# Two bank sets for the mLSTM numerators, output weights converted ahead of use, a three-stage input pipeline and later state products in a hybrid attention and mLSTM layer

## The reference

```python
h = rmsnorm(x, norm_g)
proj = h @ w_in                       # 2048 x 6672: aq ak av az | mq mk mv mo mz gates
# group A: 8 query heads on 2 key/value heads of 128, rmsnorm of q and k, axial rotary,
#          softmax(q k^T / sqrt(128)) v, times silu(az)
# group B: 4 mLSTM heads (q, k: 128, v: 256), chunks of 128 tokens, forward and backward;
#   num = (q k^T * w) v + si * (q C);  den = rowsum + si * (q n)
#   hd  = num / max(|den|, exp(-m));   C = sc * C + (we * k)^T v   # carried from chunk to chunk
#   out = rmsnorm(sigmoid(mo) * (h_fwd + h_bwd)) * silu(mz)
y = x + concat(attn_out, mlstm_out) @ w_out
```

## Time and profile before

| | |
|---|---|
| median of 3 runs | 4331.28 us (4330.11 to 4801.69) |
| the profiled execution | 4339.0 us |
| its slowest core, core 1, first to last instruction | 4337.9 us (the 8 cores: 4309.4 to 4337.9) |
| TensorE | busy 4015.4 us (93%), 24102 matmuls |
| VectorE | busy 1935.2 us (45%) |
| ScalarE | busy 1719.7 us (40%) |
| GpSimd | busy 884.8 us (20%) |
| mean granted TensorE clock of core 1 | 0.987 |
| converting weight loads issued in the first attention, at | 174, 294, 298, 455 and 584 us |
| first matmul of the first state stage, at | 708.7 us |

### The profile page before, as it was taken

One profiled execution on the slowest core, in us unless ns is written; L12 is line 12 of the kernel. 1 busy time (PEld: TensorE's weight loads), 2 busy tenths in 40 slices (PEclk: granted clock), 3 DMA queues, 4 the chain that ended last, 5 costly groups with the idle time before them and its releaser, 6 DMA issues.

```text
span 4337.9 us, 73087 instructions; the slowest of 8 cores (4309.4 to 4337.9 us)
## 1 busy us (share of the span) xinstructions
PE 4015.4 (93%) x24102; PEld 2072.3 (48%) x24102; DVE 1935.2 (45%) x4944; ACT 1719.7 (40%) x3706; POOL 884.8 (20%) x1137
## 2 busy tenths in 40 slices
PE   4799998888997999999988999999999999999999
PEld 2454444455553445445455445444544545555544
DVE  3554453543552245445444554434544444445511
ACT  4555565444330015555644443101555553333300
POOL 2533321211110024333010110003433301001100
PEclk9999999999998999999999999999999999999999
DMA  7630224463428851111032211574111100110165
GB/s 168 118 64 16 54 39 98 108 151 93 79 36 208 192 163 44 32 35 36 30 98 101 80 45 42 160 206 137 40 34 35 34 20 21 40 38 22 50 175 164
DMA packets 200369, 358.41 MB, mean 83 GB/s; under 512 B 42688, under 2 KB 129088, under 8 KB 186944
## 3 DMA queue, kind: packets, MB, share of 16 engines
q1 hardware_dynamic: 123632, 318.01, 23.9%
q0 software_dynamic: 76368, 35.72, 7.0%
HBM read 286.64 MB, written 102.76 MB: 90 GB/s over the span
## 4 chain that ended last, share of the span: by engine, by line
PE 66%; DVE 10%; issue 9%; ACT 6%; DMA 5%; POOL 3%; DVEq 1%; SPq 0%; ACTq 0%; POOLq 0%
PE PP L1163 14%; PE PP L688 10%; PE PP L738 8%; PE PP L764 7%; PE PP L751 7%; PE PP L939 6%; PE PP L980 6%; PE PP L1073 2%; PE PP L796 2%; DMA arena<-xnd 2%; POOL stats L1093 2%; DVE arena L1013 2%; DVE arena L1083 2%; DVE arena L1025 2%; DMA xnd<-arena 1%
## 5 line engine op out<-in xcount | busy, mean ns | idle before, releaser
L745 ACT ACTIVATE arena<-PP 128x1024 bf16<-128x1024 f32 x768 | 771.3, 1025 | 145.0 <-PE PP L738 143.5
L1073 PE MATMUL PP<-WR,hT 128*128 128x512 bf16 x3072 | 718.4, 382 | 0.0
L1163 PE MATMUL PP<-WR,mixT 128*128 128x512 bf16 x3072 | 674.9, 381 | 0.0
L688 PE MATMUL PP<-WR,hT 128*128 128x512 bf16 (+1 forms) x3072 | 573.2, 329 | 17.5 <-DMA WR<-w_in 17.5
L1163 PEld LDWEIGHTS PP<-WR,mixT 128*128 128x128 bf16 x3072 | 300.4, 98 | 356.9 <-issue 7.2
L751 PE MATMUL PP<-arena,mixT 128*128 128x512 bf16 x1536 | 457.8, 380 | 6.8 <-DVE arena L808 4.5
L738 PE MATMUL PP<-mixT 128*128 128x512 bf16 x1536 | 457.8, 380 | 3.3 <-ACT arena L745 2.6
L1073 PEld LDWEIGHTS PP<-WR,hT 128*128 128x128 bf16 x3072 | 296.0, 98 | 294.4 <-issue 10.6
L764 PE MATMUL PP<-hT,WR 128*128 128x512 bf16 x1536 | 410.1, 380 | 17.5 <-DVE arena L772 14.1
L688 PEld LDWEIGHTS PP<-WR,hT 128*128 128x128 bf16 x3072 | 298.1, 98 | 249.0 <-issue 25.2
L980 PE MATMUL PP<-WR,hT 128*128 128x256 bf16 x3072 | 370.8, 276 | 0.0
(11 more groups left out here) (131 smaller groups left out, 4700.0 us busy)
## 6 DMA issues: line engine op xcount, KB each, us to landing
arena<-x SPq DMA_DIRECT2D x192, 256.0 KB, 4.7
y<-arena SPq DMA_DIRECT2D x192, 256.0 KB, 5.2
mixT<-x SPq DMA_DIRECT2D x32, 1024.0 KB, 7.7
arena<-c_rope SPq DMA_DIRECT2D x192, 128.0 KB, 2.0
WR<-w_in POOLq DMA_DIRECT2D x20, 1024.0 KB, 16.0
arena<-x SPq DMA_DIRECT2D x16, 1024.0 KB, 7.3
xnd<-arena SPq DMA_DIRECT2D x32, 512.0 KB, 2.9
arena<-xnd SPq DMA_DIRECT2D x32, 512.0 KB, 7.5
```

The lines of the kernel that those rows point to most:

```text
L688: S.group('pe', [(lambda kc=kc: P.matmul(pv[:, 0:ncol], hT[:, kc, T * 128:(T + 1) * 128], W[:, kc, c0:c0 + ncol], start=(kc == 0), stop=(k ...
L745: S.op('act', lambda: A.activation(PT[t % NPT].ap, spair[t % 2][:, 0:1024], AF.Exp, scale=128.0 ** -0.5), reads=spn[t % 2], writes=[PT[t % ...
L1073: S.group('pe', [(lambda kc=kc: P.matmul(bank(b), hT[:, kc, csl(c)], W[:, kc, 0:512], start=(kc == 0), stop=(kc == KC - 1))) for kc in ran ...
L1163: S.group('pe', [(lambda kc=kc: P.matmul(bank(b), mixT[:, kc, csl(T)], W[:, kc, 0:512], start=(kc == 0), stop=(kc == KC - 1))) for kc in r ...
```

## The change

The edits, in the order of the program:

- **Output weights.** Four transfers on GpSimd's queue, device memory to device memory, write `wd['OUT0']` to `wd['OUT3']` in bfloat16 during the first sequence's attention, 60 us of model time apart. All sequences then load them on SyncE's queue. The converting loads into `WR` and the four stores of OUT blocks are gone.
- **Constants.** `norm_g` and `mlstm_norm_g` come transposed by the host, so that each partition reads one run and not single 4-byte elements; they are issued ahead of x, the others behind the third tile.
- **Input stage.** Five tiles of x and three normalised ones in flight; `tile_a` keeps the square sum, `tile_b` the scaling, one tile later; the second half of the scaling moves from ScalarE to VectorE.
- A one-column tanh at the very start.
- **Attention.** In the last head pair the gate path's product alternates between B6 and B7 from its sixth block; the transposes of a `qkv_unit` come 1000 ns of model time later.
- **States.** `state(c)` comes 3000 ns after its unit (2600 and 1300 for the last two), not 1300.
- **Outputs, banks.** `numer(c)` uses `PP[c % 2]`. To make room, the score product and the state product share B4, in one group, and the transposes of `fin` share B5.
- **Outputs, order.** The product after the power (`f4`) comes 2000 and not 1200 ns after it, the transposes 3600 and not 4000 ns after that.

```diff
-                if tag[1] == 0:
+                if tag[1] == 0 and tag[0][:3] != 'OUT':
                     S.dmas('pool', [(WR[slot][:, :, o:o + ncol], src[:, :, c0:c0 + ncol])
...
-            if tag[1] == 0 and nseq > 1 and tag[0] not in wsaved:
+            if tag[1] == 0 and nseq > 1 and tag[0] not in wsaved and tag[0][:3] != 'OUT':
...
-            S.dmas('sp', [(cb[:], c_bf[:]), (ccol[:], c_col[:]),
-                          (gcol[:], norm_g.rearrange("o (kc p) -> p (o kc)", p=128))], writes=['const'], sem='cst',
-                   allow_slow_non_contiguous=True)
+            S.dmas('sp', [(ccol[:], c_col[:]), (cb[:], c_bf[:]), (gcol[:], norm_g[:])], writes=['const'], sem='cst')
...
-        xin = [carve('ar', 8192 * i, [128, D], F32) for i in range(3)]
-        xn0 = [carve('ar', 24576 + 4096 * i, [128, D], BF16) for i in range(2)]
+        xin = [carve('ar', 8192 * i, [128, D], F32) for i in range(3)] + [carve('mx', 8192 * i, [128, D], F32) for i in range(2)]
+        xn0 = [carve('ar', 24576 + 4096 * i, [128, D], BF16) for i in range(2)] + [carve('mx', 16384, [128, D], BF16)]
...
-            S.op('act', lambda: A.activation(dst.ap[:, cs], src.ap[:, cs], AF.Copy, scale=st[:, 4 + b:5 + b]),
+            S.op(eng, (lambda: A.activation(dst.ap[:, cs], src.ap[:, cs], AF.Copy, scale=st[:, 4 + b:5 + b])) if eng == 'act' else
+                 (lambda: V.tensor_scalar(dst.ap[:, cs], src.ap[:, cs], st[:, 4 + b:5 + b], None, ALU.mult)),
...
-                F.after(dl + 3300, done)
+                F.after(dl + (4300 if spread else 3300), done)
...
-                return ring[nring[0] % 2] if cur[0] < 3 else 6
+                return ring[nring[0] % 2] if cur[0] < 3 or zn[0] > 4 else 6
...
+            if s_ == 0:
+                for n in range(4):
+                    F.after(60000 + 60000 * n, lambda n=n: S.dma('pool', wd['OUT%d' % n], w_out_v[:, :, 512 * n:512 * n + 512],
+                                                                 writes=['DOUT%d' % n], sem='cv%d' % n))
...
-                    F.after(1300, lambda: state(c))
+                    F.after(3000 if c > 2 else (2600 if c == 2 else 1300), lambda: state(c))
...
             def front(c):
                 i = c % 2
-                S.op('pe', lambda: P.matmul(bank(4)[:, 0:128], kTm.ap[:, csl(c)], qTm.ap[:, csl(c)], start=True, stop=True),
...
+                fns = [lambda: P.matmul(bank(4)[:, 0:128], kTm.ap[:, csl(c)], qTm.ap[:, csl(c)], start=True, stop=True)]
...
+                if c > 0:
+                    fns.append(lambda: P.matmul(bank(4)[:, 128:385], kxf.ap[:, c - 1, :], vext.ap[:, c - 1, :], start=True, stop=True))
...
+                if c > 0:
+                    fstate(c - 1)
...
             def numer(c):
                 i = c % 2
                 qs = qTm.ap[:, csl(c)]
+                pN = PP[i]
+                pNd = pN[:, :].rearrange("p (d e) -> p d e", d=2)
+                bns = ['B%d' % (2 * i), 'B%d' % (2 * i + 1)]
...
-                    tp = bankb(2 + i)
+                    tp = bankb(5)
...
-                F.chain((100, f0), (700, f1), (600, f2), (800, f3), (1200, f4), (4000, f5))
+                F.chain((100, f0), (700, f1), (600, f2), (800, f3), (2000, f4), (3600, f5))
...
                 if c + 1 < NT:
                     front(c + 1)
-                    fstate(c)
                 numer(c)
...
                 def tile_a(T):
-                    i = T % 2
-                    rms(xin[T % 3], xn0[i], i)
-                    rms2(i)
-                    rms3(xin[T % 3], xn0[i], i, 0)
-                    rms3(xin[T % 3], xn0[i], i, 1)
-                    if T + 3 < NT:
-                        pa_load(T + 3)
+                    rms(xin[T % 5], xn0[T % 3], T % 2)
+                    rms2(T % 2)
+
+                def tile_b(T):
+                    rms3(xin[T % 5], xn0[T % 3], T % 2, 0)
+                    rms3(xin[T % 5], xn0[T % 3], T % 2, 1, 'dve')
+                    if T + 5 < NT:
+                        pa_load(T + 5)
...
                     if T + 2 < NT:
-                        tile_a(T + 2)
+                        tile_b(T + 2)
+                    if T + 3 < NT:
+                        tile_a(T + 3)
                     unit(T)
```

76 lines of the change are left out of this document (42 added, 34 removed).

## The result

The changed kernel takes 4193.06 us in the median (4189.3 to 4436.11, 4 runs): 0.968 of the time before, 95% interval 0.965 to 0.971. That is 3.2% less; 4.4% was forecast. The profiled execution took 4189.3 us, its slowest core, core 6, 4188.2. In some executions the cores of a die run at a lower clock and the time is longer (here the 4436.11); ratios leave these out.

A forecast was written before the change was run, and what follows sets the result against it. TensorE, busy 93% of the span, bounds the kernel, so its idle stretches were priced: -52 + 4 - 108 - 40 + 9 + 0 - 5 = -192, from a median of 4331.3 to 4139 us; range 4100 to 4195.

The forecast's parts named there:

- Output weights, -52: First sequence's output projection: takes the second's length, 237 for 289 us, without converting loads and stores; bounds 43 and 52.
- the conversions cost little: Four weight conversions during the first sequence's attention: +4 us, 1 us each; bounds 0 and 62.
- the rival of a slow one: Weight conversions: one is slow and later weight blocks wait; over 165 us each the kernel is slower than before; chance 0.02.
- Outputs, -108: Twelve mLSTM output stages: TensorE sets the pace at 4.16 us a chunk, VectorE's loop 4.04; 808 us against 916.
- The shared B4 costs nothing: Output stages: B4's readers head VectorE's loop and the next product comes a chunk later, so sharing costs 0.
- State products, -40: State stages with prenorm: issuing products one unit of 16 matmuls later covers the mean wait for value copies; bounds 20 and 64.
- Input stage, +9: First sequence's first pass: deeper buffers do not shorten a tile, L470 lengthens its chain; 11 tiles x 1.2 less 4.
- ScalarE, which is relieved, is not on this chain: Input stage: moving half the scaling off ScalarE does not shorten the chain of a tile.
- The chain breaks: Rival for the input stage: the power is ready early, a tile takes some 5 us, -35 for +9, total 4095; chance 0.07.
- The start, 0: First matmul's wait for the first weight block: more x tiles cost 10, fewer single-element transfers give back; between -10 and +10.
- Attention, -5: Attention's gate path: 14.1 us of waiting for VectorE's L772, three of the last head pair's eight blocks now alternate.
- the rival in which VectorE keeps the output loop and half the gain stays away: Output stages: VectorE's loop still sets the pace, half the gain is lost, total 4193 us; chance 0.13.

The follow-up runs named there:

- f2_old_order: Changed kernel with the old gate-chain delays (1200 and 4000 for 2000 and 3600), both bank pairs kept; output stages 937.8 us, ratio 0.999 to the kernel before.
- g3_input_order: Changed kernel with L458 of tile T+3 issued into tile T's matmuls, L462 and L464 only after them; first pass 94.0 us, ratio 0.959 to the kernel before.
- f3_x_behind_weights: Changed kernel with first loads of input tiles 3 and 4 held until the first weight block landed; start 36.4 us, ratio 0.964 to the kernel before.

## Why the prediction was right and where it was wrong

In the mean over the cores the span fell by 144.1 us, and the stages add up to it: start +3.6, pass and attention of the first sequence +1.7, of the other two -2.5, output projections -45.6, states +8.0, outputs -109.3. The forecast was -192. The states account for all 48 us of the difference; that the other terms come to -152 in both is partly luck.

- **Output weights, -52:** right. The two stretches differ by 3 us, the first is 51 shorter on the slowest core (46 in the mean over the cores). That the conversions cost little was right too: pass and attention of the first sequence together are 1.7 us longer, the pass alone 2.8. The four conversions took 14.8 us in the median from issue to landing and none over 39.3, so the rival of a slow one is out.
- **Outputs, -108:** right in size (-109.3 over the cores) and in mechanism. A chunk was put at 4.16 and takes 4.18, VectorE's loop at 4.04 and takes 4.13. "The shared B4 costs nothing" was wrong by 0.19 us in VectorE's loop, which still stayed under TensorE's. That the size fits is partly luck: it includes the 8.8 us lost in the openings, and the last two chunks of a stage take 3.90 and 3.56 us and not 4.16. That a second set of banks alone gains nothing held in f2_old_order. What I did not see is that the order alone would do nearly all of it.
- **State products, -40: this step failed.** It came out as +1.4 with `prenorm`, +6.6 without, and 8.8 more in the stages that follow. The text took the delay for a distance: "one unit of 16 matmuls more". A later place in the queue is a distance only if the instruction does not thereby pass another write to what it reads. Here it passed the next chunk's copy, which shares a key with its own. With a key of its own the same delay gave 24.6 us against the changed kernel and 23.2 against the kernel before (432.1 to 408.9), inside the forecast's bounds of 20 to 64 and short of its 40. The larger part of the late copies was ScalarE's wait for the store, 43.7 us, which the prediction named as what stays and did not price. "Bounds: 20" was itself wrong: the lower bound had to be zero or a loss.
- **Input stage, +9:** it came out as +2.8. The chain was right in L464 ahead of L683 and L462 behind the evictions. Two things were not. L470 takes 0.74 us in the rows, not 1.2. And "ScalarE, which is relieved, is not on this chain" was wrong: before, the evictions waited behind L675 for ScalarE's L650, and they now start 0.55 us earlier, which takes back most of L470. Ten tiles in the middle of the pass take 9.0 us in the mean on the slowest core (8.2 before), inside the 8.5 to 9.1 forecast, but with stretches of lower clock in them; at full clock a tile takes 7.97. The Trainium skill, VectorE: DVE Perf Modes, section The perf-mode tier table, has the figure from which the prediction's estimate of 0.7 for L470 was worked out, and the trace agrees with that and not with my nearest row, which reads its operand from PSUM. "The chain breaks" (-35) did not come from deeper buffers; g3_input_order, 28.7 us under the kernel before, shows that it comes from the order.
- **The start, 0:** +3.6, inside its bounds. Transfers of x do cost the block time, 3.0 us for each of the five tiles that f3_x_behind_weights took away. The Trainium skill, DMA: Bandwidth & Descriptors, section Queues, rings and completion order, has the engines take turns between queues; f3_x_behind_weights agrees in direction; by it the start was to be +10, and it is +3.6. I should have counted the tiles issued until the block lands: six before, eight after.
- **Attention, -5:** the other two sequences' pass and attention are 1.8 and 0.7 us shorter, the first one's attention 1.1.

The time that came out, 4193, is to the microsecond that of the rival in which VectorE keeps the output loop and half the gain stays away. The chunk of 4.18 us rules this rival out, and so does the sum of the output stages. A total that fits a rival is not evidence for it; the stage is.

## What to carry to other kernels

Before you move an instruction later to give its input more time, list what writes between the old and the new place, and ask whether the dependency tracker can tell those writes from the one awaited; keys coarser than the tiles turn distance into nothing. Compare both engines' loops per chunk: two delays that set the order of the queues were worth 134 us here, a second pair of banks 14. And cost a stall by the clock that follows it as well as by its own length.

## What the runs showed of the hardware

Two waits of TensorE of 1.0 and 1.2 us, with three small matmuls about them, were followed by a granted clock of 0.50 for the next 3 us; the sixteen matmuls behind them took 5.30 us instead of 3.62. In 60 of 96 openings of another run, with waits of 0.9 and 1.2 us, it did not fall, and in 9 of 96 of the changed kernel's own. So such a stall costs 2.2 or 3.9 us, and which of the two the rows ahead of it did not tell me.

Between f2_old_order and the changed kernel no instruction differs, only the order in the queues of VectorE and TensorE, and the times are 3% apart.

On VectorE, L1032 started 0.90 to 0.91 us behind the first of the two scalings L1021 that read the same bank; before the change, with a bank of its own, the same update started 0.72 us behind. No run varies the bank alone.
